# A fused inference step on one core: the decode attention packs two sequences into each 32-row tile, and the memory attention runs in two head halves with a softmax each

## The reference, cut to what matters

```
proj = rmsnorm(x) @ w_in            # pool channels | q | k | v, 512 columns each
A = causal multi-scale pooling of the pool channels, @ w_pool
B = softmax(q . k) v                # 8 heads x 64; decode: 256 cached keys of its own + its new key
x = x + concat(A, B) @ w_out
m = rmsnorm(mem_prompt); mk = m @ w_ck; mv = m @ w_cv    # memory of the prompt, 256 rows
x = x + softmax((rmsnorm(x) @ w_cq) . mk) mv @ w_co      # 4 heads x 256; decode: cached memory K/V of each sequence
x = x + relu(rmsnorm(x) @ w_up)^2 @ w_down
y = rmsnorm(x)
```

## Time and profile before

| | us |
|---|---|
| median of 3 runs (449.13 to 451.85) | 450.35 |
| span of the profiled execution | 447.9 |
| PE busy in it | 423.8 (95%) |
| DVE busy | 266.7 (60%) |
| ACT busy | 229.5 (51%) |
| POOL busy | 39.1 (9%) |

### The profile page before, as it was taken

The page is one execution under the profiler, slowest core; times in us unless marked ns, Lnnn a source line. Parts: engine busy times, 40 slices in busy tenths (PEclk is TensorE's granted clock), DMA queues, the critical chain, the costliest instruction groups (busy, mean ns, idle before and its releaser), DMA issues.

```text
span 447.9 us, 8424 instructions
## 1 busy us (share of the span) xinstructions
PE 423.8 (95%) x3346; PEld 393.0 (88%) x3346; DVE 266.7 (60%) x417; ACT 229.5 (51%) x411; POOL 39.1 (9%) x49
## 2 busy tenths in 40 slices
PE   2699899999999999999999999999999999999992
PEld 2699787787988999795599999999999999999992
DVE  2676787889454587654316967766666633444304
ACT  5777657664355474434026746656666533353202
POOL 0621001450000030000002200000000000020000
PEclk9979999999999999999989999999999999999998
DMA  7899897485699887597716655555555555545002
GB/s 273 286 280 343 324 265 240 161 283 170 185 352 317 334 277 284 173 368 281 266 36 246 235 190 187 189 190 189 187 187 184 186 180 176 176 168 179 1 1 97
DMA packets 42409, 96.80 MB, mean 216 GB/s; under 512 B 3954, under 2 KB 20466, under 8 KB 42234
## 3 DMA queue, kind: packets, MB, share of 16 engines
q1 hardware_dynamic: 40962, 93.03, 60.9%
q10 hardware_dynamic: 1408, 3.23, 1.9%
HBM read 91.94 MB, written 4.54 MB: 215 GB/s over the span
## 4 chain that ended last, share of the span: by engine, by line
PE 77%; ACT 8%; DVE 7%; issue 3%; DMA 2%; POOL 2%; ACTq 0%; SPq 0%; DVEq 0%; POOLq 0%
PE psum L865 68%; PE psum L666 4%; ACT w_hi L881 2%; DVE w_lo L1080 2%; DMA raw<-in_w_in 2%; POOL ssq L1306 1%; ACT swapped L881 1%; PE psum L791 1%; PE psum L778 1%; ACT soft L1024 1%; ACT act_hi L881 1%; DVE soft L1191 1%; PE psum L813 1%; DVE stats L1194 1%; PE psum L686 0%
## 5 line engine op out<-in xcount | busy, mean ns | idle before, releaser
L1080 DVE TENSOR_TENSOR w_lo<-raw,w_hi 128x1024 fp32r<-128x1024 f32 x82 | 103.1, 1268 | 90.5 <-ACT w_hi L881 90.0
L865 PE MATMUL psum<-act_hi,w_hi 128*128 128x264 f32 (+1 forms) x416 | 122.5, 294 | 9.0 <-DVE act_lo L1084 8.0
L881 ACT ACTIVATE w_hi<-raw 128x1024 fp32r<-128x1024 f32 x82 | 85.5, 1054 | 76.3 <-PE psum L865 64.2
L865 PE MATMUL psum<-act_lo,w_hi 128*128 128x264 f32 (+1 forms) x416 | 119.7, 288 | 0.0
L865 PE MATMUL psum<-act_hi,w_lo 128*128 128x264 f32 (+1 forms) x416 | 119.5, 287 | 0.0
L865 PEld LDWEIGHTS psum<-act_hi,w_hi 128*128 128x128 f32 x416 | 80.2, 193 | 12.9 <-DVE w_lo L1080 8.3
L865 PEld LDWEIGHTS psum<-act_lo,w_hi 128*128 128x128 f32 x416 | 80.0, 192 | 0.2
L865 PEld LDWEIGHTS psum<-act_hi,w_lo 128*128 128x128 f32 x416 | 79.8, 192 | 0.0
L1306 POOL TENSOR_TENSOR ssq<-ssq,sq 128x264 f32<-128x264 f32 (+1 forms) x31 | 25.4, 818 | 339.5 <-ACT sq L902 337.0
L865 PE MATMUL psum<-hid_hi,w_hi 128*128 128x264 f32 x176 | 50.1, 284 | 0.0
L865 PE MATMUL psum<-hid_lo,w_hi 128*128 128x264 f32 x176 | 50.1, 284 | 0.0
(11 more groups left out here) (155 smaller groups left out, 769.1 us busy)
## 6 DMA issues: line engine op xcount, KB each, us to landing
raw<-in_w_down SPq DMA_DIRECT2D x20, 512.0 KB, 3.3
raw<-in_w_up SPq DMA_DIRECT2D x18, 512.0 KB, 4.3
raw<-in_w_in SPq DMA_DIRECT2D x16, 512.0 KB, 5.4
raw_more<-in_w_up SPq DMA_DIRECT2D x14, 512.0 KB, 4.4
raw_more<-in_w_down SPq DMA_DIRECT2D x12, 512.0 KB, 4.2
keysT<-in_cache_k SPq DMA_DIRECT2D x16, 256.0 KB, 4.4
stage<-in_cache_v SPq DMA_DIRECT2D x16, 256.0 KB, 4.1
raw<-in_w_ck SPq DMA_DIRECT2D x8, 512.0 KB, 5.2
```

Source lines behind the costliest of these rows:

```text
L865: mm = pe.matmul(out, a, b, start=first and m == 0, stop=end_ and m == 2)
L881: return nc.scalar.activation(out, in_, ACT.Copy, scale=scale)
L1080: V.tensor_tensor(lo_of(c), raw_of(c), hi_of(c).bitcast(F32), ALU.subtract).then_inc(w_lo_ready, 1)
```

## The change: what it does

- The two decode halves share one tile. A 32-row strip now serves two sequences: sequence j and sequence j+4 have rows of their own in it (8 each for the keys, 2 each for the memory). `cS(0)` and `cS(1)` accumulate into one bank with one softmax at the end; likewise `cO(0)` and `cO(1)`. Table `CLOSER` maps the first of such a pair to the second, and the bank is held from the first to the second.
- One `cP_T`, one `ownp`, one matmul with `ownp`, one `opart` and one `c_attn` (4 matmuls with 8 columns) in place of two each. The probabilities go to a tile `own_q`, zeroed by POOL, in which each sequence's columns stand apart and the other's are zero.
- The memory attention is split by head half instead of by sequences: `xS(half, 0)` and `xS(half, 1)` share a bank and have a softmax of 256 columns, followed by `xc_T(half)`, `xc_O(half, 0)`, `xc_O(half, 1)`, `xc_attn(half)` (4 matmuls; before, 8 for each b).
- Jobs stand behind other chunks, `softT` has 4 slots instead of 5, `plan_banks` lets a pair hold any bank, and the loads follow the new places. `make_qblock` is two DVE instructions of half the size.

The number of strip matmuls stays: 32 for `cS`, 64 for `xS`, 16 for `cO`, 32 for `xc_O`.

```diff
-SOFT_TS = 5
+SOFT_TS = 4
@@ plan_jobs
-    put(v_end + 1, ("v_nat", 0), ("v_nat", 1), ("v_nat", 2), ("cP_T", 0), ("m_tile", 0), ("m_tile", 1))
+    put(v_end + 1, ("v_nat", 0), ("v_nat", 1), ("v_nat", 2), ("m_tile", 0), ("m_tile", 1))
     put(v_end + 2, ("P_T", 2), ("P_T", 3), ("O", 0), ("m_tile", 2), ("m_tile", 3))
     put(v_end + 3, ("S", 4), ("S", 5), ("m_tile", 4), ("m_tile", 5))
-    put(u_end, ("cO", 0), ("cS", 1), ("O", 1), ("m_tile", 6), ("m_tile", 7))
-    put(u_end + 1, ("P_T", 4), ("P_T", 5), ("c_attn", 0))
-    put(u_end + 2, ("cP_T", 1), ("S", 6), ("S", 7))
+    put(u_end, ("cS", 1), ("O", 1), ("m_tile", 6), ("m_tile", 7))
+    put(u_end + 1, ("P_T", 4), ("P_T", 5))
+    put(u_end + 2, ("S", 6), ("S", 7))
     put(u_end + 3, ("O", 2), ("stat", "m"), ("stat_col", "m"))
-    put(u_end + 4, ("differences",))
-    put(u_end + 5, ("P_T", 6), ("P_T", 7))
-    put(u_end + 6, ("cO", 1), ("O", 3), ("pool", 0), ("pool", 1))
-    put(u_end + 7, ("pool", 2), ("pool", 3), ("c_attn", 1))
+    put(u_end + 4, ("cP_T",), ("differences",))
+    put(u_end + 5, ("cO", 0), ("P_T", 6), ("P_T", 7))
+    put(u_end + 6, ("O", 3), ("pool", 0), ("pool", 1))
+    put(u_end + 7, ("pool", 2), ("pool", 3))
+    put(u_end + 9, ("cO", 1))
+    put(u_end + 10, ("c_attn",))
...
-    put(a + 3, ("xP_T", 0), ("xP_T", 1))
-    put(b, ("xP_O", 0), ("xP_O", 1), ("xP_S", 2), ("xS", 1, 0), ("xS", 1, 1), ("xP_T", 2), ("xP_S", 3), ("xP_O", 2),
-        ("xc_T", 0), ("xc_T", 1), ("xP_T", 3), ("xc_O", 0, 0), ("xc_O", 0, 1), ("xP_O", 3),
-        ("xc_O", 1, 0), ("xc_attn", 0), ("xc_O", 1, 1), ("xc_attn", 1))
+    put(a + 3, ("xP_T", 0), ("xP_T", 1), ("xc_T", 0))
+    put(b, ("xP_S", 2), ("xc_O", 0, 0), ("xP_O", 0), ("xP_O", 1), ("xS", 1, 0), ("xS", 1, 1), ("xP_S", 3), ("xc_O", 0, 1), ("xc_attn", 0))
+    put(b + 1, ("xP_T", 2), ("xc_T", 1), ("xP_T", 3))
+    put(b + 2, ("xP_O", 2), ("xc_O", 1, 0), ("xP_O", 3), ("xc_O", 1, 1), ("xc_attn", 1))
@@ plan_banks: the bank of a pair is held, and given back to the common choice at the pair's second job
+            if j in OPENER:
+                jobs[j] = jobs[OPENER[j]]
+                held.discard(jobs[j][0])
                 continue
...
+            if j in CLOSER:
+                taken |= of_groups(c, CHUNK_OF[CLOSER[j]])
+            bank = min(set(range(8)) - taken - held, key=lambda b: stamp[b])
@@ PE, cO
-                    pe.matmul(B, ownp[:, :], v_nat[0:DEC, 2, :], start=True, stop=False, skip_group_check=True)
+                    pT = by_sequence(own_q, b)
+                    if b == 0:
+                        wait_out(pe, ("cP_T",))
+                        wait_out(pe, ("v_nat", 2))
+                        pe.matmul(B, ownp[:, :], v_nat[0:DEC, 2, :], start=True, stop=False, skip_group_check=True)
@@ PE, xc_attn
-                    for half in range(2):
-                        wait_out(pe, ("xc_O", b, half))
-                        for f in range(AT):
-                            last = pe.matmul(B[:, 4 * (AT * half + f):4 * (AT * half + f) + 4], opart[:, OPART["xc_O", b, half] % 2, f * P:(f + 1) * P], con("rowsel"), start=True, stop=True)
+                    half = i[0]
+                    wait_out(pe, ("xc_O", half, 1))
+                    for f in range(AT):
+                        last = pe.matmul(B[:, DEC * f:DEC * (f + 1)], opart[:, OPART["xc_O", half, 1] % 2, f * P:(f + 1) * P], con("mine_x"), start=True, stop=True)
@@ DVE: the first job of a pair closes what is open and does nothing else
-                    if job[0] == "xS" and job not in SOFT:
+                    if job in CLOSER:
```

More of the change, by code:

```diff
@@ L189 @@
 ORDER = [j for c in range(-1, NC) for j in JOBS[c]]
+CHUNK_OF = {j: c for c in JOBS for j in JOBS[c]}
+CLOSER = {("cS", 0): ("cS", 1), ("cO", 0): ("cO", 1)}
+CLOSER |= {(what, half, 0): (what, half, 1) for what in ("xS", "xc_O") for half in range(2)}
+OPENER = {closer: opener for opener, closer in CLOSER.items()}
 def plan_banks():
-    jobs, groups, uses, stamp, now = {}, {}, [0] * 8, [-1] * 8, 0
-    hold_from, hold_to = ORDER.index(("xS", 0, 0)), ORDER.index(("xS", 1, 1))
+    jobs, groups, uses, stamp, held, now = {}, {}, [0] * 8, [-1] * 8, set(), 0
     def take(bank):
@@ L204, in take, with of_groups @@
         return uses[bank] - 1
+    def of_groups(c, d):
+        return {bank for g, *_ in CHUNKS[c:d + 2] for bank in banks_of(g)}
     for c, (g, w, n, k, last) in enumerate(CHUNKS):
@@ L212, in plan_banks @@
                 continue
-            if j[0] == "xS" and j != ("xS", 0, 0):
-                jobs[j] = jobs["xS", 0, 0]
+            if j in OPENER:
+                jobs[j] = jobs[OPENER[j]]
+                held.discard(jobs[j][0])
                 continue
[L216 to L219, removed]
+            taken = set(banks_of(g)) if not last else set() if g + 1 == len(GROUPS) else set(banks_of(g + 1))
+            if (w, n) == ("cq", 1) and last and ORDER.index(j) < ORDER.index(("xS", 1, 0)):
+                taken = set()
+            if j in CLOSER:
+                taken |= of_groups(c, CHUNK_OF[CLOSER[j]])
+            bank = min(set(range(8)) - taken - held, key=lambda b: stamp[b])
+            if j in CLOSER:
+                held.add(bank)
             jobs[j] = (bank, take(bank))
@@ L233 @@
 HI = turns(("O", "c_attn", "pool", "xP_O", "xc_attn"))
[L234 to L243, removed]
+SOFT = {j: i for i, j in enumerate(j for j in ORDER if j[0] in ("S", "xP_S") or j[0] in ("cS", "xS") and j in OPENER)}
+SOFT_T = turns(("P_T", "xP_T"))
+SOFT_END = {("S", h): ("P_T", h) for h in range(NH)} | {("cS", 1): ("cP_T",)}
+SOFT_END |= {("xP_S", h): ("xP_T", h) for h in range(MH)} | {("xS", h, 1): ("xc_T", h) for h in range(2)}
+SOFT_T_END = {("P_T", h): ("O", h // 2) for h in range(NH)} | {("xP_T", h): ("xP_O", h) for h in range(MH)}
+SOFT_OF = {t: s for s, t in SOFT_END.items()}
+OPART = {("cO", 1): 0, ("xc_O", 0, 1): 1, ("xc_O", 1, 1): 2}
+OPART_END = {("cO", 1): ("c_attn",), ("xc_O", 0, 1): ("xc_attn", 0), ("xc_O", 1, 1): ("xc_attn", 1)}
+PARTS = {j: i for i, j in enumerate(j for j in ORDER if j in CLOSER)}
 def before(turn_of, job, slots):
@@ L611, in load @@
                         wait_full(sp, ("cS", 1))
[L612 removed]
+                    sp.dma_start(mem_keys(unit), ins["mem_k"][s, half]).then_inc(done, 16)
                 else:
@@ L671, in run @@
                     return
-                if job != ("xS", 0, 1) and job != ("xS", 1, 0) and job != ("xS", 1, 1):
+                if job not in OPENER:
                     begin(job)
@@ L1025, in run @@
                     last.then_inc(exp_ready if what == "S" else free, 1)
-                elif what in ("P_T", "cP_T", "xP_T", "xc_T"):
+                elif what in ("cP_T", "xc_T"):
+                    wait_full(act, job)
+                    act.wait_ge(zeros_ready, 1 if what == "cP_T" else 2)
+                    if job == ("xc_T", 1):
+                        wait_full(act, ("xc_O", 0, 1))
+                    tile, heads = (own_q, NH) if what == "cP_T" else (own_x, 2)
+                    copy(own_rows(tile, heads), rows_of(B, heads)).then_inc(t_copied if what == "cP_T" else free, 1)
+                elif what in ("P_T", "xP_T"):
                     n = SOFT_T[job]
```

146 lines of the change are left out of this document (77 added, 69 removed).

## The result

| | before | after |
|---|---|---|
| median of 4 runs, us | 450.56 (449.13 to 451.85) | 457.81 (456.88 to 458.80) |
| span of the profiled execution, us | 447.9 | 455.1 |
| `S(0)` starts, us into the span | 47.42 | 46.01 |
| from there to `xP_S(0)` | 131.55 | 141.07 |
| from there to the last `stat` matmuls before `up` | 80.32 | 79.03 |

The account below looks back on a forecast made before the run. PE was taken as the bound, with DVE and ACT a few tenths apart from it up to 102 us. First stage +7.1 and second 0 gave 450.35 + 7.1 = 457.4 us, range 453.0 to 460.5.

Parts of the forecast that it names:

- PE work that goes: First stage, chunks 10 to 25: one cP_T, one ownp matmul and one c_attn fewer on PE, 2.55 us.
- DVE and ACT: First stage: dropped softmax, copy and opart save 2.4 us; exponential of cS(1) ends at 83.4 instead of 85.8.
- The wait that comes in its place: Before O(1): PE, done with cS(1) at 77.4, waits for its exponential until 83.4, a pause of 6.0 us.
- The clock: After the pause before O(1): PE's clock falls to half, 2.8 us lost; bounds 0 and 2.8.
- The second wait: Before cP_T: PE waits 2.2 us for mkT, which comes 1.9 later; 3.4 us without the clock's loss.
- Sum of the first stage: Chunks 10 to 25: 6.25 - 1.05 + 1.9 = +7.1 us, or +5.5 without the clock's loss.
- the second fall: Rival: the clock falls again in the pause before cP_T, 1.3 to 2.8 us more, 459 to 460; chance 0.15.
- with the first loss it is under 2.9: Argument against another clock fall before cP_T: the pause is shorter than the 2.9 us from stop to fall seen earlier.
- The second stage: 196 to 231 us: 3.1 us saved against 3.0 of new waits, -0.1; taken as 0, bounds -1.5 to +1.5.
- All of the 2.4 us that DVE and ACT had won is eaten by the pause: First stage: their gain does not shorten the time, since from the pause before O(1) on they wait for PE.

Follow-up runs that it names:

- e_bank: Changed kernel with O(1) in bank 7 instead of the bank of cS(0) and cS(1); 452.9 us, ratio 1.009.
- b_bank: Kernel before, with only O(1) put into the bank of cS(1); 456.1 us, ratio 1.012.
- e_end: Changed kernel with xc_O(0, 1) ahead of xP_S(3) and xc_O(1, 1) ahead of xP_O(3); 455.0 us, ratio 1.011.
- e_end2: Changed kernel, second stage reordered: xc_O(0, 1) ahead of xS(1, 1), xc_attn(0) of xP_S(3), xc_O(1, 0) and xc_O(1, 1) of xP_O(2), xc_attn(1) of xP_O(3); 450.7 us.
- e_clk3: Changed kernel with 15 matmuls that nobody reads filling the pause before O(1); 456.3 us, ratio 1.015.
- e_cpt: Changed kernel with cP_T moved one chunk forward, behind chunk 18; 454.0 us, ratio 1.011.
- e_loads: Changed kernel with loads of the first four sequences' keys back behind chunks 7 to 10; 458.8 us, ratio 1.022.

## Why the prediction was right, and where it was not

The forecast was 457.4 and the result 457.81. The mechanism is the one given, a wait on `soft` for a shared bank with half clock behind it and a second wait on `mkT`. That the number is within 0.4 us is luck: +2.4 us in the first stage meets -1.3 in the second and -1.4 at the start. The numbers below are in the frame of the kernel before: 1.4 us are added to times of the changed trace, since its `S(0)` is that much earlier.

- *PE work that goes*: the records are gone as counted. *DVE and ACT*: the exponential of `cS(1)` ended at 82.4 + 1.4 = 83.8, against 83.4; they won 2.0 us and not 2.4.
- *The wait that comes in its place*: 7.0 us against 6.0, in front of `O(1)`, on ACT's `soft`. PE was 0.5 us earlier at it than forecast and ACT 0.4 later. e_bank, in which the wait goes with the bank, and b_bank, in which it comes with the bank alone, show that the shared bank is the cause.
- *The clock*, first fall: 5.6 us at half after PE had gone on, 2.8 lost, as taken from the earlier trace rows. In e_end and e_end2 it was 3.8 us behind the same pause, so the agreement to a tenth is chance. e_clk3, in which the clock stays up and PE reaches `cP_T` 2.15 us sooner after `O(1)`, shows that this time was real and reached `cP_T`.
- *The second wait*: 2.4 us against 2.2; `mkT` 2.2 us later against 1.9. e_cpt shows it.
- *Sum of the first stage*: +7.1 forecast, +9.5 measured. The term that was missing is the second fall, 1.7 us in this trace, which stood among the rivals with 0.15. The argument against it ("with the first loss it is under 2.9") took a single fall, 2.9 us after a stop, for a bound. The clock fell 4.1 us after PE had stopped, when PE was at work again. The rest, 0.7, is small: `mkT` came 0.3 later than forecast, from its release to `P_T(6)` PE took 0.2 more, and behind `P_T(6)` 0.8 us went where 1.05 were forecast.
- *The second stage*: 0 forecast, -1.3 measured, where 1.7 is the fall of the clock that the kernel before had there. The forecast did not look at the granted clock of this stretch. The waits for `opart` were 1.5 and 0.9 (1.45 and 0.8), those for `mix_lo` 0.7 twice, as forecast. That they bring the clock down in many executions was in no term.
- *The start*, -1.4 us, was in no term; 1.1 of it is the shorter fall of the clock there, and e_loads leaves a few tenths at most for the loads. So +2.4, -1.3 and -1.4 cancel, and 0.4 us at the end stay unexplained: the stretch from the last `stat` to the end took 189.0 in all 12 profiled executions with the changed code and 188.6 in the two without.
- *All of the 2.4 us that DVE and ACT had won is eaten by the pause*: true for the changed kernel. But e_bank showed what the forecast had not: with the pause gone, DVE is not free either, because its two `w_lo` begin inside POOL's sums again.

## What to carry to other kernels

When two jobs share a bank or a tile, look at who takes that bank next: a rule that picks the bank taken longest ago counts from the first of the pair, and hands a bank on just when its result is still waiting to be read. Price a wait on PE as the wait and a chance of half clock behind it, also for waits of 0.7 to 2.5 us and also after PE has resumed, and look at the granted clock of every stretch whose time is forecast, in the kernel before too. An idea is not judged by its first schedule: here the same shared tiles were 1.8% slower or 1.3% faster than the kernel before, by the order of some ten jobs and the bank of one.
